# Conditioning vectors of a two-block transformer: from a TensorE product with a turn to a VectorE sum over weight blocks, closed by a product with ones

## The chip, the cores and the metric

One core of one Trainium2 chip runs the whole program. The metric is the device time of one launch in microseconds, the median of a few launches. The profile is of one more execution.

## The reference

The program runs a first block (four feed-forward layers around a pooling mixer and a differential attention) and then a second block (a Mamba mixer and an attention). The part that the change touches feeds the second block. Each of its two layers is modulated by vectors made from two conditioning vectors, one for the latent and one for the context rows:

```python
sc, scc = jax.nn.silu(c), jax.nn.silu(c_ctx)
for i in range(DEPTH):                                   # DEPTH = 2
    sh, scl, gt = jnp.split(sc @ mod_w[i] + mod_b[i], 3, axis=-1)
    shc, sclc, gtc = jnp.split(scc @ mod_w[i] + mod_b[i], 3, axis=-1)
    in_lat = rmsnorm_2(h_lat, norm_w[i]) * (1.0 + scl[:, None]) + sh[:, None]
    in_ctx = rmsnorm_2(h_ctx, norm_w[i]) * (1.0 + sclc) + shc
```

`c` and `c_ctx` have 1024 numbers, `mod_w[i]` is 1024 x 3072 in float32. So it is two rows times a matrix of 6144 columns in all: 25 MB of weights, each read once. Nothing before the Mamba mixer needs the result. The feed-forward layer that hides it is `h + 0.5 * (silu(n @ up_a) * (n @ up_b)) @ down`, with 512 rows and a hidden width of 2816.

## The kernel before

**Streams.** All large weights come through one stream of 438 units of 128 x 1024 float32 (512 KB, one block column of eight 128 x 128 blocks). SyncE loads a unit into one of two buffers `raw`; ScalarE copies it rounded into one of four buffers `wh` (`split`, line 1091); GpSimd computes the rest `wl = raw - wh` (line 392, one 128 x 1024 operation for each unit); TensorE then does three products for each block (high x high, high x low, low x high; `project`, line 469, 24 matmuls of 512 columns for a unit). Each engine runs its own instruction list in order. Semaphores connect them.

**The feed-forward loop.** The hidden width is done in parts of 8, 8 and 6 blocks. Over the blocks of a part runs a loop of w // 2 passes, with two pairs (`jj` = 0, 1) in each pass. A pair is two units: gate and value. So a pass with w = 8 has four units. The order on the engines in a pass is:

- TensorE: wait for `gated` (a PSUM bank is free), unit of the gate (unit 0 or 2 of the pass), unit of the value (unit 1 or 3);
- ScalarE: silu of the gate (line 1139), the splits of the units that take the places of the two just used, wait for `gated`, then the high half `fh` (line 1143);
- VectorE: wait for silu and for the value, product into `tmp` (line 1616, which signals `gated`), wait for `fh`, low half `fl` (line 1618).

Then the down projection of the part reads `fh` and `fl`, and line 1641 adds it to `x`.

**The modulation.** It rides in the loops of the first two parts of feed-forward layers 0, 1 and 2: 3 x 2 x 4 = 24 passes, each making 256 of the 6144 columns, for both rows. ScalarE issues two loads of 512 KB into `modw[:, 0]` and `modw[:, 1]` at the head of a pass (line 1137), after a wait that the buffers are free. In the second pair TensorE multiplies, between the two units, the eight 128-row chunks of the weights with the silu of the conditioning vectors (`csil`, padded to 32 columns), in four column groups of the array (line 516). VectorE copies the 128 x 256 result to `modst` (line 1603). Behind the last unit of the pass TensorE turns it into columns with two products against a selector `modsel` (line 525), which also adds the four groups. After the second part VectorE adds the bias to the 32 columns of the layer and stores them in `modv` (line 1627).

A float32 product counts as two TensorE instructions in the profile (line 516: 384 for 192 calls; line 525: 96 for 48), the rounded ones of `project` as one.

`link` is VectorE's own chain: `link.mark(ins)` lets an instruction count up a semaphore and `link.until(n)` waits for that count, so that an operation sees what an earlier one on the same engine wrote.

Of the kernel before, what the change touches and what calls it, by code (L numbers as in the profile page):

```python
# [27 lines left out]
P = 128  # L28
# [34 lines left out]
for _name, _n in STAGE_UNITS:  # L63
# [8 lines left out]
    ("m_d", 32), ("diff_lambda", 256), ("slopes", 8), ("pool_rcount", 64), ("modsel", 2),  # L72
]
COL = {}
NCOL = 0
# [34 lines left out]
def at(base, i=None, per=0):  # L110

    return base if i is None else i * per + base
# [7 lines left out]
def build(nc, A, ctx):  # L120
    def sb(name, shape, dt=FP32, scope=ctx):
        return scope.enter_context(nc.sbuf_tensor(name, shape, dt))

    def sem(name):
        return ctx.enter_context(nc.semaphore(name))
# [26 lines left out]
    with scope() as first:  # L152
        hh = sb("hh", [P, KD, T], F32R, first)
        hl = sb("hl", [P, KD, T], F32R, first)
        fh = sb("fh", [P, KD, T], F32R, first)
        fl = sb("fl", [P, KD, T], F32R, first)
        dist = sb("dist", [P, T], scope=first)
        csil = sb("csil", [P, KD, 32], scope=first)
        modw = sb("modw", [P, 2, UNIT], scope=first)
        mk = sb("mk", [P, 2 * X_HEADS, TC], scope=first)  # L160
        mv = sb("mv", [P, 2 * X_HEADS, 2, P], scope=first)
        with scope() as s:
            dq = sb("dq", [P, 2, T], scope=s)
            dk = sb("dk", [P, 2, T], scope=s)
            dv = sb("dv", [P, 2, T], scope=s)
            dvt = sb("dvt", [P, NB, P], scope=s)
            de = sb("de", [P, 2, 2, T], scope=s)
            dw = sb("dw", [P, T], scope=s)
            dT = sb("dT", [P, NB, T], scope=s)
            dnm = sb("dnm", [P, 2, 2], scope=s)  # L170
            drs = sb("drs", [P, 2, 2], scope=s)
            drr = sb("drr", [P, 2, 2], scope=s)
            drl = sb("drl", [P, 1], scope=s)
            lamt = sb("lamt", [P, 2, 64], scope=s)
            lams = sb("lams", [P, 2], scope=s)
            lame = sb("lame", [P, 2], scope=s)
            lam = sb("lam", [P, 1], scope=s)
            dgain = sb("dgain", [P, 1], scope=s)
        xoh = sb("xoh", [P, X_HEADS, T], F32R, first)
        xol = sb("xol", [P, X_HEADS, T], F32R, first)  # L180
        qx = sb("qx", [P, X_HEADS, T], scope=first)
        with scope() as s:
            ubuf = sb("ubuf", [P, 2, PAD + T], scope=s)
            sg = ubuf[:, :, 0:T]
            modst = sb("modst", [P, 2 * P], scope=s)
# [90 lines left out]
    s_init = sem("init")  # L276
    c_silu = sem("c_silu")
    mod_loaded = [sem(f"mod_loaded{s}") for s in range(2)]
    mod_acc, mod_staged = sem("mod_acc"), sem("mod_staged")
    mod_turned, mod_read, gmod_ready = sem("mod_turned"), sem("mod_read"), sem("gmod_ready")  # L280
# [52 lines left out]
    X0 = 2  # L333
# [123 lines left out]
    def _(pe):  # L457
# [48 lines left out]
                last = nc.tensor.matmul(B[6][:, chunk(c)], rstd[:, c:c + 1].to_broadcast([P, P]), ident, start=True, stop=True)  # L506
            last.then_inc(rb_ready, 1)

        def modulation(n, i):

            for s in range(2):
                pe.wait_ge(mod_loaded[s], at(16 * (n + 1), i, 16))
            for kk in range(2):
                for j in range(4):
                    k = 2 * j + kk
                    last = nc.tensor.matmul(B[6][32 * j:32 * j + 32, 2 * P:4 * P], csil[:, k, :],
                                            modw[:, k // 4, (k % 4) * 2 * P:(k % 4 + 1) * 2 * P],
                                            start=(kk == 0), stop=(kk == 1))
            last.then_inc(mod_acc, 1)

        def modulation_turn(n, i):

            pe.wait_ge(mod_staged, at(n + 1, i, 1))
            for h in range(2):
                last = nc.tensor.matmul(B[6][:, bass.ds(i * 4 + (4 * n + 2 * h) % 32 + 32 * (n // 8), 2)], modst[:, chunk(h)],
                                        col("modsel", 0, 2), start=True, stop=True)
            last.then_inc(mod_turned, 1)

        def ffn(f, name, norm, following):
            n = NORM[norm]  # L530
# [3 lines left out]
            for p, w in enumerate(FF_PARTS):  # L534
                def arrive(k):
                    pe.wait_ge(h_ready, 8 * n + k + 1)
                with pe.Fori(0, w // 2) as i:
                    for jj in range(2):

                        pe.wait_ge(gated, at(pairs + jj + 1, i, 2))  # L540
                        g = u + 2 * jj
                        project(g, hh, hl, [(B[2 * jj][:], 0, T)], i, 4, arrive=arrive if p == 0 and jj == 0 else None)
                        if w == KD and f < 3 and jj == 1:
                            modulation(8 * f + 4 * p, i)
                        project(g + 1, hh, hl, [(B[2 * jj + 1][:], 0, T)], i, 4)
                        if w == KD and f < 3 and jj == 1:
                            modulation_turn(8 * f + 4 * p, i)
                u += 2 * w
                done = xr(f, MIXERS_BEFORE[name]) + 8 * p
                hidden = pairs + w  # L550
# [532 lines left out]
    def _(act):  # L1083
# [41 lines left out]
        def ffn(f, name, norm_name, following, ready):  # L1125
# [3 lines left out]
            for p, w in enumerate(FF_PARTS):  # L1129
                with act.Fori(0, w // 2) as i:  # L1130
                    for jj in range(2):
                        g = u + 2 * jj
                        if w == KD and f < 3 and jj == 0:
                            n = 8 * f + 4 * p
# [303 lines left out]
        nc.scalar.activation(csil[:, :, 0:2], col("c", 0, 16).rearrange("p (k c) -> p k c", c=2), ACT.Silu).then_inc(c_silu, 1)  # L1438
# [122 lines left out]
    def _(dve):  # L1561
# [35 lines left out]
                    rest(k - 1)  # L1597
            rest(KD - 1)

        def modulation(n, i):  # L1600

            dve.wait_ge(mod_acc, at(n + 2, i, 1))
            nc.vector.tensor_copy(modst[:], B[6][:, 2 * P:4 * P]).then_inc(mod_staged, 1)

        def ffn(f, name, norm_name, gain):
            norm(norm_name, x, T, gain)
# [1 line left out]
            pairs = f * sum(FF_PARTS)  # L1608
            for p, w in enumerate(FF_PARTS):
                with dve.Fori(0, w // 2) as i:  # L1610
                    for jj in range(2):
                        if w == KD and f < 3 and jj == 1:
                            modulation(8 * f + 4 * p, i)
                        dve.wait_ge(silu_ready, at(pairs + jj + 1, i, 2))
                        dve.wait_ge(unit_done, at(u + 2 * jj + 2, i, 4))
                        nc.vector.tensor_tensor(tmp[:, jj, :], sg[:, jj, :], B[2 * jj + 1][:], ALU.mult).then_inc(gated, 1)  # L1616
# [2 lines left out]
                                                fh[:, bass.ds(i * 2 + jj, 1), :].bitcast(FP32), ALU.subtract)\  # L1619
                          .then_inc(hid_lo, 1)  # L1620
                        dve.wait_ge(hid_lo, at(pairs + jj + 1, i, 2))
                u += 2 * w

                if p == 1 and f < 3:

                    dve.wait_ge(mod_turned, 8 * (f + 1))
# [372 lines left out]


        nc.vector.memset(eps6[:], 1e-6)
        nc.vector.memset(csil[:], 0.0)
        nc.vector.memset(eps5[:], 1e-5).then_inc(s_init, 1)
        free = 0
        for signal, banks in ((gated, 2), (x_ready, X0), (kv_ready, 2), (kv_copied, 4), (mod_acc, 1)):
# [261 lines left out]
    return blocks  # L2267


def modulation_units(w):  # L2270

    w = w.reshape(2, 2, 4, P, 12, 2 * P).transpose(0, 4, 1, 3, 2, 5)
    return np.ascontiguousarray(w.reshape(48, P, UNIT))


# [44 lines left out]
```

## Time and profile before

| | us |
|---|---|
| median of 3 runs | 3976.95 (3973.89 to 3977.0) |
| profiled execution, its own time | 3973.89 |
| its span, first to last instruction | 3972.1 |

| engine | busy us | share |
|---|---|---|
| TensorE, matmul | 3600.4 | 91% |
| TensorE, weight load | 2925.1 | 74% |
| VectorE | 1547.8 | 39% |
| ScalarE | 1351.7 | 34% |
| GpSimd | 1245.0 | 31% |

The mean granted clock of TensorE is 0.938 of full speed. A row of the timeline gives the start of an instruction (or of a run of the same ones, with their count) and its duration; matmuls overlap, so the distance from start to start is the time that one costs. "Idle before" is how long the engine had stood still, and the name behind it who released it.

### The profile page before, as it was taken

To read this page: it belongs to the slowest core of one execution; us is meant where nothing else is said; L and a number is where in the kernel's file an instruction comes from. 1 tells how busy PE (TensorE), PEld (TensorE's weight loads), DVE (VectorE), ACT (ScalarE), POOL (GpSimd) and SP (SyncE) were. 2 spreads that over 40 slices of the span, in tenths; PEclk is the share of its full clock that TensorE was granted. 3 is DMA by queue.
4 is the path that set the end of the run, shared out by engine and by line. 5 is a ranking of instruction groups with operands and counts; after the bars stand their busy time and mean duration, and the time that the engine had idled before them with its cause. 6 is when DMAs were issued, how large, how long until landed. Compare 5 with 4: busy or idle time off the path is not lost.

```text
span 3972.1 us, 50085 instructions
## 1 busy us (share of the span) xinstructions
PE 3600.4 (91%) x17896; PEld 2925.1 (74%) x17896; DVE 1547.8 (39%) x2368; ACT 1351.7 (34%) x2246; POOL 1245.0 (31%) x683
## 2 busy tenths in 40 slices
PE   6999998999999998887999977899889897779998
PEld 6788876788878886565788866888878886646667
DVE  1322263322232224564322233665566665444442
ACT  3322233322232224444322233334333333324443
POOL 4244432344434442221244413333333423100001
PEclk9899999999999999998999979999999998779999
DMA  4333221233233321111122210100110101100001
GB/s 157 120 111 111 95 75 53 105 126 112 91 107 126 111 95 59 53 58 37 58 95 95 95 51 32 43 33 32 37 37 32 42 32 57 34 6 22 21 21 38
DMA packets 72964, 269.76 MB, mean 68 GB/s; under 512 B 8096, under 2 KB 8096, under 8 KB 72096
## 3 DMA queue, kind: packets, MB, share of 16 engines
q1 hardware_dynamic: 64944, 236.14, 17.8%
q10 hardware_dynamic: 7920, 32.25, 2.2%
q8 instruction: 68, 1.11, 0.1%
q14 instruction: 32, 0.26, 0.0%
HBM read 264.16 MB, written 4.19 MB: 68 GB/s over the span
## 4 chain that ended last, share of the span: by engine, by line
issue 46%; PE 29%; POOL 17%; DVE 5%; ACT 2%; POOLq 1%; ACTq 0%; DVEq 0%
POOL wl L392 15%; PE ps L469 13%; PE ps L915 2%; PE ps L897 2%; PE ps L482 1%; PE ps L924 1%; PE ps L494 1%; PE ps L483 1%; PE ps L484 1%; PE ps L784 1%; PE ps L797 1%; PE ps L834 1%; POOL xs L417 1%; DVE rstd L1791 1%; PE ps L898 1%
## 5 line engine op out<-in xcount | busy, mean ns | idle before, releaser
L392 POOL TENSOR_TENSOR wl<-raw,wh 128x1024 fp32r<-128x1024 f32 x438 | 1055.8, 2411 | 2585.0 <-ACT wh L1091 2585.0
L1091 ACT ACTIVATE wh<-raw 128x1024 fp32r<-128x1024 f32 x438 | 463.0, 1057 | 1200.2 <-PE ps L469 537.6
L469 PE MATMUL ps<-hh,wh 128*128 128x512 f32 (+1 forms) x1856 | 740.7, 399 | 30.7 <-DVE hl L1586 30.0
L469 PE MATMUL ps<-hl,wh 128*128 128x512 f32 (+1 forms) x1856 | 722.0, 389 | 0.0
L469 PE MATMUL ps<-hh,wl 128*128 128x512 f32 (+1 forms) x1856 | 721.9, 389 | 0.0
L469 PEld LDWEIGHTS ps<-hh,wh 128*128 128x128 f32 x1856 | 356.1, 192 | 140.6 <-issue 49.8
L469 PEld LDWEIGHTS ps<-hh,wl 128*128 128x128 f32 x1856 | 356.2, 192 | 75.0
L469 PEld LDWEIGHTS ps<-hl,wh 128*128 128x128 f32 x1856 | 357.4, 193 | 68.4 <-issue 1.7
L482 PE MATMUL ps<-fh,wh 128*128 128x512 f32 x768 | 306.3, 399 | 3.1 <-DVE fl L1618 3.0
L484 PE MATMUL ps<-fh,wl 128*128 128x512 f32 x768 | 300.8, 392 | 0.0
L483 PE MATMUL ps<-fl,wh 128*128 128x512 f32 x768 | 300.0, 391 | 0.0
L1616 DVE TENSOR_TENSOR tmp<-ubuf,ps 128x512 f32<-128x512 f32 x88 | 60.6, 689 | 600.4 <-PE ps L469 600.4
L1618 DVE TENSOR_TENSOR fl<-tmp,fh 128x512 f32 x88 | 206.9, 2351 | 92.6 <-ACT fh L1143 92.6
L469 PE MATMUL ps<-mh,wh 128*128 128x512 f32 (+1 forms) x768 | 217.8, 365 | 7.2 <-ACT cvin L1264 4.0
L1641 DVE SCALAR_TENSOR_TENSOR x<-ps,x 128x512 f32 (+1 forms) x96 | 65.6, 691 | 404.5 <-PE ps L484 404.5
L469 PE MATMUL ps<-ml,wh 128*128 128x512 f32 (+1 forms) x768 | 201.6, 344 | 0.0
L469 PE MATMUL ps<-mh,wl 128*128 128x512 f32 (+1 forms) x768 | 200.5, 343 | 0.0
L482 PEld LDWEIGHTS ps<-fh,wh 128*128 128x128 f32 x768 | 144.9, 189 | 34.4 <-DVE fl L1618 4.7
L484 PEld LDWEIGHTS ps<-fh,wl 128*128 128x128 f32 x768 | 144.4, 188 | 33.0
L483 PEld LDWEIGHTS ps<-fl,wh 128*128 128x128 f32 x768 | 144.7, 188 | 30.4
L1139 ACT ACTIVATE ubuf<-ps 128x512 f32<-128x512 f32 x88 | 52.6, 597 | 320.2 <-PE ps L469 320.2
L494 PE MATMUL ps<-sq,sqr 128*128 128x1 f32 x736 | 120.2, 294 | 33.7 <-ACT sqr L1098 33.3
(313 smaller groups left out, 5515.7 us busy)
## 6 DMA issues: line engine op xcount, KB each, us to landing
raw<-stream_dram SPq DMA_DIRECT2D x438, 512.0 KB, 3.2
modw<-mod_dram ACTq DMA_DIRECT2D x48, 512.0 KB, 3.6
x<-xT_dram SPq DMA_DIRECT2D x1, 2048.0 KB, 8.4
side<-ctxT_dram ACTq DMA_DIRECT2D x2, 1024.0 KB, 7.4
park_dram<-x ACTq DMA_DIRECT2D x1, 2048.0 KB, 8.4
x<-park_dram ACTq DMA_DIRECT2D x1, 2048.0 KB, 7.7
out_dram<-x SPq DMA_DIRECT2D x8, 256.0 KB, 2.2
side<-memT_dram SPq DMA_DIRECT2D x1, 1024.0 KB, 4.8
```

The source lines that it names most:

```text
L392: nc.gpsimd.tensor_tensor(wl[:, u % RING, :], raw[:, u % RAW, :], wh[:, u % RING, :].bitcast(FP32), ALU.subtract).then_inc(s_lo, 1)
L469: last = nc.tensor.matmul(bank, a[:, s, w], b[:, k, c0:c1], start=(k == 0 and a is wh and b is hi), stop=(k == KD - 1 and a is wl))
L482: nc.tensor.matmul(bank, wh[:, s, w], hi, start=start, stop=False)
L483: nc.tensor.matmul(bank, wh[:, s, w], lo, start=False, stop=False)
L484: last = nc.tensor.matmul(bank, wl[:, s, w], hi, start=False, stop=stop)
L494: last = nc.tensor.matmul(B[7][:, KD * c + k:KD * c + k + 1], sqr[:, k % 2, chunk(c)], ones[:, 0:1], start=True, stop=True)
L897: nc.tensor.matmul(ps[:, o:o + T], queries, kcur[h, to, 0:T], start=True, stop=True)
L915: last = nc.tensor.matmul(B[1][64 * r:64 * r + 64, b * P:(b + 1) * P], vcur2[:, k, :], pT2[:, s % 2, k, :], start=(k == 0), stop=(k == NCH ...
L1091: nc.scalar.activation(wh[:, u % RING, :], raw[:, u % RAW, :], ACT.Copy).then_inc(s_hi, 1)
L1616: nc.vector.tensor_tensor(tmp[:, jj, :], sg[:, jj, :], B[2 * jj + 1][:], ALU.mult).then_inc(gated, 1)
L1618: nc.vector.tensor_tensor(fl[:, bass.ds(i * 2 + jj, 1), :], tmp[:, jj:jj + 1, :], fh[:, bass.ds(i * 2 + jj, 1), :].bitcast(FP32), ALU.subt ...
L1641: nc.vector.scalar_tensor_tensor(x[:, m, :], B[4 + slot][:].unsqueeze(1), 0.5, x[:, m, :], ALU.mult, ALU.add).then_inc(x_ready, 1)
```

## The change

The modulation moves from products on TensorE to VectorE, and its weights are laid out in other units. For each block of 128 columns (48 of them, two in a pass) VectorE multiplies the eight 128 x 128 weight blocks each with one number for each partition and adds them up, once for each of the two rows: 16 operations of 128 x 128 for a block of columns, of which the first two are multiplications and the other 14 multiply-adds onto `modp`. TensorE adds over the partitions with one product against a column of ones for each row. In the pass:

- TensorE's products between the two units of the second pair are gone. Behind the last unit it waits twice for `mod_part`, each time for one block of columns, and does two products behind each wait.
- VectorE's copy to `modst` is gone. The 32 operations of a pass stand behind line 1618 of the first pair and ahead of line 1616 of the second. An operation waits for the one before last.
- ScalarE's wait ahead of the two loads is for `mod_used`, TensorE's last product of the pass before.

The amount loaded is the same, two units of 512 KB in a pass. `csil` loses its padding, its memset and its 32 columns.

```diff
 # TensorE
-        def modulation(n, i):
-            for s in range(2):
-                pe.wait_ge(mod_loaded[s], at(16 * (n + 1), i, 16))
-            for kk in range(2):
-                for j in range(4):
-                    k = 2 * j + kk
-                    last = nc.tensor.matmul(B[6][32 * j:32 * j + 32, 2 * P:4 * P], csil[:, k, :],
-                                            modw[:, k // 4, (k % 4) * 2 * P:(k % 4 + 1) * 2 * P],
-                                            start=(kk == 0), stop=(kk == 1))
-            last.then_inc(mod_acc, 1)
-        def modulation_turn(n, i):
-            pe.wait_ge(mod_staged, at(n + 1, i, 1))
-            for h in range(2):
-                last = nc.tensor.matmul(B[6][:, ...], modst[:, chunk(h)],
-                                        col("modsel", 0, 2), start=True, stop=True)
-            last.then_inc(mod_turned, 1)
+        def modulation(v, i):
+            pe.wait_ge(mod_part, at(2 * v + 2, i, 4))
+            for r in range(2):
+                last = nc.tensor.matmul(B[6][:, bass.ds(i * 4 + (2 * v + r), 1)], modp[:, v % 2, r, :], ones[:, 0:1],
+                                        start=True, stop=True)
+            last.then_inc(mod_used, 1)
...
                         project(g, hh, hl, [(B[2 * jj][:], 0, T)], i, 4, arrive=...)
-                        if w == KD and f < 3 and jj == 1:
-                            modulation(8 * f + 4 * p, i)
                         project(g + 1, hh, hl, [(B[2 * jj + 1][:], 0, T)], i, 4)
                         if w == KD and f < 3 and jj == 1:
-                            modulation_turn(8 * f + 4 * p, i)
+                            modulation(16 * f + 8 * p, i)
+                            modulation(16 * f + 8 * p + 1, i)
     # ScalarE
-                            act.wait_ge(mod_acc, at(n + 1, i, 1))
+                            act.wait_ge(mod_used, at(v + 2, i, 2))
                             for r in range(2):
-                                act.dma_start(modw[:, r:r + 1, :], A["mod"][at(2 * n + r, i, 2)].unsqueeze(1)).then_inc(mod_loaded[r], 16)
+                                act.dma_start(modw[:, r:r + 1, :], A["mod"][at(v + r, i, 2)].unsqueeze(1)).then_inc(mod_loaded[r], 16)
     # VectorE
-        def modulation(n, i):
-            dve.wait_ge(mod_acc, at(n + 2, i, 1))
-            nc.vector.tensor_copy(modst[:], B[6][:, 2 * P:4 * P]).then_inc(mod_staged, 1)
+        def modulation(v, i):
+            dve.wait_ge(mod_loaded[v % 2], at(16 * (v // 2 + 1), i, 16))
+            dve.wait_ge(mod_used, at(v + 1, i, 2))
+            done = {}
+            for k in range(KD):
+                for r in range(2):
+                    to, block, c = modp[:, v % 2, r, :], modw[:, v % 2, chunk(k)], csil[:, k, r:r + 1]
+                    if k:
+                        link.until(done[r])
+                        ins = nc.vector.scalar_tensor_tensor(to, block, c, to, ALU.mult, ALU.add)
+                    else:
+                        ins = nc.vector.tensor_scalar(to, block, c, None, ALU.mult)
+                    if k < KD - 1:
+                        done[r] = link.mark(ins)
+                    else:
+                        ins.then_inc(mod_part, 1)
...
                     for jj in range(2):
-                        if w == KD and f < 3 and jj == 1:
-                            modulation(8 * f + 4 * p, i)
                         dve.wait_ge(silu_ready, ...)
                         dve.wait_ge(unit_done, ...)
                         nc.vector.tensor_tensor(tmp[:, jj, :], sg[:, jj, :], B[2 * jj + 1][:], ALU.mult).then_inc(gated, 1)
...
+                        if w == KD and f < 3 and jj == 0:
+                            modulation(16 * f + 8 * p, i)
+                            modulation(16 * f + 8 * p + 1, i)
     # weights
-        "mod": modulation_units(I["mod_w_2"]),
+        "mod": units(outputs_first(I["mod_w_2"][0], 0, 24) + outputs_first(I["mod_w_2"][1], 0, 24)),
```

## Rows read from the trace of the kernel before

**Rows 1.** The page's first part: busy us (share of the span) xinstructions of each engine.

```profile
PE 3600.4 (91%) x17896; PEld 2925.1 (74%) x17896; DVE 1547.8 (39%) x2368; ACT 1351.7 (34%) x2246; POOL 1245.0 (31%) x683
```

**Rows 2.** Waits: engine line <- releaser: us in total, times, longest us.

```profile
DVE tmp L1616 <- PE ps L469: 600.4, 88, 10.2
```

**Rows 3.** Timeline of TensorE, first modulation: start us, us, line, [idle before <-releaser].

```profile
137.36 1.07 PE L516 MATMUL ps<-modw,csil 128*32 128x256 f32 x16
138.36 0.50 PE L469 MATMUL ps<-hh,wh 128*128 128x512 f32 x1
...
143.97 0.50 PE L525 MATMUL ps<-cols,modst 128*128 128x2 f32 x4
144.33 0.48 PE L469 MATMUL ps<-hh,wh 128*128 128x512 f32 x1
```

**Rows 4.** Timeline of VectorE over one pass of the first feed-forward loop.

```profile
131.97 0.69 DVE L1616 TENSOR_TENSOR tmp<-ubuf,ps 128x512 f32<-128x512 f32 x1 [6.55 <-PE ps L469]
133.71 2.35 DVE L1618 TENSOR_TENSOR fl<-tmp,fh 128x512 f32 x1 [1.06 <-ACT fh L1143]
...
144.17 0.69 DVE L1616 TENSOR_TENSOR tmp<-ubuf,ps 128x512 f32<-128x512 f32 x1 [5.25 <-PE ps L469]
...
155.62 0.69 DVE L1616 TENSOR_TENSOR tmp<-ubuf,ps 128x512 f32<-128x512 f32 x1 [7.35 <-PE ps L469]
```

**Rows 5.** Timeline of GpSimd over the same pass.

```profile
133.11 2.40 POOL L392 TENSOR_TENSOR wl<-raw,wh 128x1024 fp32r<-128x1024 f32 x1 [2.45 <-ACT wh L1091]
139.09 2.41 POOL L392 TENSOR_TENSOR wl<-raw,wh 128x1024 fp32r<-128x1024 f32 x1 [3.58 <-ACT wh L1091]
145.31 2.41 POOL L392 TENSOR_TENSOR wl<-raw,wh 128x1024 fp32r<-128x1024 f32 x1 [3.81 <-ACT wh L1091]
```

**Rows 6.** Timeline of ScalarE, the split behind the pass's last unit.

```profile
144.17 1.06 ACT L1091 ACTIVATE wh<-raw 128x1024 fp32r<-128x1024 f32 x1 [5.16 <-PE ps L469]
```

**Rows 7.** Timeline of VectorE, a pass of the loop that carries no modulation.

```profile
1409.99 0.69 DVE L1616 TENSOR_TENSOR tmp<-ubuf,ps 128x512 f32<-128x512 f32 x1 [10.18 <-PE ps L469]
...
1431.97 0.69 DVE L1616 TENSOR_TENSOR tmp<-ubuf,ps 128x512 f32<-128x512 f32 x1 [6.89 <-PE ps L469]
```

**Rows 8.** Groups by shape, VectorE: xcount | busy us, mean ns | idle before.

```profile
L1732 DVE SCALAR_TENSOR_TENSOR dw<-de,drr 128x128 f32<-128x128 f32 x8 | 2.8, 351 | 0.6
L1729 DVE TENSOR_SCALAR de<-de,drl 128x128 f32<-128x128 f32 x8 | 2.3, 286 | 0.3
```

**Rows 9.** Timeline of VectorE, differential attention: unchained ops, then a chained pair.

```profile
1533.99 0.61 DVE L1714 SCALAR_TENSOR_TENSOR de<-dist,cols,ps 128x128 f32<-128x128 f32 x2 [12.85 <-PE ps L655]
...
1571.64 0.16 DVE L1728 TENSOR_TENSOR drl<-drr,lam 128x1 f32<-128x1 f32 x1
1571.83 0.28 DVE L1729 TENSOR_SCALAR de<-de,drl 128x128 f32<-128x128 f32 x1
```

**Rows 10.** Timeline of VectorE, the convolution taps, each waiting for the op before last.

```profile
2656.50 1.01 DVE L1915 SCALAR_TENSOR_TENSOR sqr<-cvin,cols,sqr 128x770 f32<-128x770 f32 x1
2657.43 3.15 DVE L1915 SCALAR_TENSOR_TENSOR tmp<-cvin,cols,tmp 128x770 f32<-128x770 f32 x1
```

**Rows 11.** Timeline of GpSimd at the same time.

```profile
2657.21 2.55 POOL L392 TENSOR_TENSOR wl<-raw,wh 128x1024 fp32r<-128x1024 f32 x1 [1.74 <-ACT wh L1091]
```

**Rows 12.** Timeline of TensorE, its matmul behind a wait.

```profile
2673.26 1.01 PE L834 MATMUL ps<-yh,wh 128*128 128x512 f32 x2 [4.72 <-DVE acc L1998]
```

**Rows 13.** Stretches: TensorE busy (xinstructions), granted clock (1.00 is full), DMA share, GB/s.

```profile
2673.20:2675.80 2.60, 2.54 (x8) 0.50 0.43 162
2675.80:2676.80 1.00, 1.00 (x6) 0.75 0.00 0
...
1651.00:1655.00 4.00, 4.00 (x11) 0.50 0.34 112
1655.00:1656.50 1.50, 1.50 (x6) 0.76 0.13 52
```

**Rows 14.** DMA issues: xcount, KB each, median us to landing.

```profile
modw<-mod_dram ACTq DMA_DIRECT2D x48, 512.0 KB, 3.6
```

More of the change, by code:

```diff
@@ L71 @@
     ("m_norm_w", 16), ("a_q_norm", 1), ("a_k_norm", 1), ("c", 16), ("dt_bias", 64), ("a_log", 64),
-    ("m_d", 32), ("diff_lambda", 256), ("slopes", 8), ("pool_rcount", 64), ("modsel", 2),
+    ("m_d", 32), ("diff_lambda", 256), ("slopes", 8), ("pool_rcount", 64),
 ]
@@ L157, in build @@
         dist = sb("dist", [P, T], scope=first)
-        csil = sb("csil", [P, KD, 32], scope=first)
+        csil = sb("csil", [P, KD, 2], scope=first)
         modw = sb("modw", [P, 2, UNIT], scope=first)
@@ L184, in build @@
             sg = ubuf[:, :, 0:T]
-            modst = sb("modst", [P, 2 * P], scope=s)
+            modp = sb("modp", [P, 2, 2, P], scope=s)
         vt = modw[:, :, 0:TC]
@@ L278, in build @@
     mod_loaded = [sem(f"mod_loaded{s}") for s in range(2)]
-    mod_acc, mod_staged = sem("mod_acc"), sem("mod_staged")
-    mod_turned, mod_read, gmod_ready = sem("mod_turned"), sem("mod_read"), sem("gmod_ready")
+    mod_part = sem("mod_part")
+    mod_used, mod_read, gmod_ready = sem("mod_used"), sem("mod_read"), sem("gmod_ready")
     sq_ready, sq_used, rt_ready = sem("sq_ready"), sem("sq_used"), sem("rt_ready")
@@ L507, in norm_spread @@
             last.then_inc(rb_ready, 1)
-        def modulation(n, i):
-            for s in range(2):
-                pe.wait_ge(mod_loaded[s], at(16 * (n + 1), i, 16))
-            for kk in range(2):
-                for j in range(4):
-                    k = 2 * j + kk
-                    last = nc.tensor.matmul(B[6][32 * j:32 * j + 32, 2 * P:4 * P], csil[:, k, :],
-                                            modw[:, k // 4, (k % 4) * 2 * P:(k % 4 + 1) * 2 * P],
-                                            start=(kk == 0), stop=(kk == 1))
-            last.then_inc(mod_acc, 1)
-        def modulation_turn(n, i):
-            pe.wait_ge(mod_staged, at(n + 1, i, 1))
-            for h in range(2):
-                last = nc.tensor.matmul(B[6][:, bass.ds(i * 4 + (4 * n + 2 * h) % 32 + 32 * (n // 8), 2)], modst[:, chunk(h)],
-                                        col("modsel", 0, 2), start=True, stop=True)
-            last.then_inc(mod_turned, 1)
+        def modulation(v, i):
[4 more added lines that the diff above has]
+            last.then_inc(mod_used, 1)
         def ffn(f, name, norm, following):
@@ L1133, in ffn @@
                         if w == KD and f < 3 and jj == 0:
-                            n = 8 * f + 4 * p
-                            act.wait_ge(mod_acc, at(n + 1, i, 1))
+                            v = 16 * f + 8 * p
+                            act.wait_ge(mod_used, at(v + 2, i, 2))
                             for r in range(2):
-                                act.dma_start(modw[:, r:r + 1, :], A["mod"][at(2 * n + r, i, 2)].unsqueeze(1)).then_inc(mod_loaded[r], 16)
+                                act.dma_start(modw[:, r:r + 1, :], A["mod"][at(v + r, i, 2)].unsqueeze(1)).then_inc(mod_loaded[r], 16)
                         act.wait_ge(unit_done, at(g + 1, i, 4))
@@ L1437, in _ @@
         act.wait_ge(consts_in, 32)
-        nc.scalar.activation(csil[:, :, 0:2], col("c", 0, 16).rearrange("p (k c) -> p k c", c=2), ACT.Silu).then_inc(c_silu, 1)
+        nc.scalar.activation(csil[:].rearrange("p k c -> p (k c)"), col("c", 0, 16), ACT.Silu).then_inc(c_silu, 1)
         norm("ffn0", x, T, lambda k: (x_in, 16))
@@ L1610, in ffn @@
                 with dve.Fori(0, w // 2) as i:
+                    link.enter(i, 2 * 2 * (KD - 1) if w == KD and f < 3 else 0)
                     for jj in range(2):
-                        if w == KD and f < 3 and jj == 1:
-                            modulation(8 * f + 4 * p, i)
                         dve.wait_ge(silu_ready, at(pairs + jj + 1, i, 2))
@@ L1621, in ffn @@
                         dve.wait_ge(hid_lo, at(pairs + jj + 1, i, 2))
+                        if w == KD and f < 3 and jj == 0:
+                            modulation(16 * f + 8 * p, i)
+                            modulation(16 * f + 8 * p + 1, i)
+                    link.leave(w // 2)
                 u += 2 * w
                 if p == 1 and f < 3:
-                    dve.wait_ge(mod_turned, 8 * (f + 1))
+                    dve.wait_ge(mod_used, 2 + 16 * (f + 1))
                     nc.vector.tensor_tensor(modv[:, 16 * f:16 * f + 16], B[6][:, 32 * f:32 * f + 32].rearrange("p (m c) -> p m c", c=2),
@@ L2001, in _ @@
         nc.vector.memset(eps6[:], 1e-6)
-        nc.vector.memset(csil[:], 0.0)
         nc.vector.memset(eps5[:], 1e-5).then_inc(s_init, 1)
         free = 0
-        for signal, banks in ((gated, 2), (x_ready, X0), (kv_ready, 2), (kv_copied, 4), (mod_acc, 1)):
+        for signal, banks in ((gated, 2), (x_ready, X0), (kv_ready, 2), (kv_copied, 4), (mod_used, 2)):
             for _ in range(banks):
@@ L2267, in weight_stream @@
     return blocks
-def modulation_units(w):
-    w = w.reshape(2, 2, 4, P, 12, 2 * P).transpose(0, 4, 1, 3, 2, 5)
-    return np.ascontiguousarray(w.reshape(48, P, UNIT))
 def kernel(**inputs):
@@ L2294 @@
         "slopes": np.tile(np.array([2.0 ** (-8.0 * (h + 1) / DIFF_HEADS) for h in range(DIFF_HEADS)], f32), (P, 1)),
-        "modsel": (np.arange(P)[:, None] % 32 == np.arange(2)[None, :]).astype(f32),
         "pool_rcount": np.tile(np.concatenate([1.0 / np.minimum(np.arange(1, 17), w) for w in POOL_WINDOWS])
```

## The prediction

> **What bounds the kernel now.** I read the engines' busy shares first: TensorE's matmuls fill 91% of the span, VectorE 39% [rows 1]. The waits say the same of the feed-forward loops: in each of its 88 pairs VectorE stands waiting for a product of TensorE, 600.4 us in all [rows 2]. So whatever TensorE is spared there is gained, and whatever it has to wait for is lost.
>
> Then the timeline of one pass with a modulation. It lasts from one first-pair product at 131.97 to the next at 155.62: 23.65 us [rows 4]. A pass of the loop that carries none takes 1431.97 - 1409.99 = 21.98 us, two pairs of 10.99 [rows 7]. The modulation thus costs TensorE 1.67 us in each of its 24 passes, 40 us in all. Of it 1.00 lies between the start of the 16 instructions at line 516 and the next matmul, and 0.36 is the same distance for the 4 instructions at line 525 [rows 3].
>
> The reader should next see what line 1618 does in that pass. It is a 128x512 subtraction with both inputs in SBUF and takes 2.35 us, ending at 136.06; line 1616, of the same size with one input in PSUM, takes 0.69 [rows 4]. GpSimd's line 392 runs from 133.11 to 135.51 [rows 5]: line 1618 starts inside it and ends 0.55 after it. A VectorE operation on two SBUF tensors stands still while GpSimd's runs. All 32 added operations have their tensors in SBUF.
>
> **Part 1, what TensorE is spared.** The 16 instructions at line 516 go (1.00 us and the 0.31 around them that is left of the 1.67). The 4 at line 525 (0.36) become 8, in two groups of 4 of the same weight shape: 0.72. If TensorE never waited, a pass would be 21.98 + 0.72 = 22.7 us, 0.95 less than now, 23 us in 24 passes. This is the most that the change can give.
>
> **Part 2, what VectorE has to do.** In a pass 4 multiplications and 28 multiply-adds of 128x128. The trace has both shapes, from SBUF with a number for each partition: 286 and 351 ns [rows 8]. What one costs in a row is less than its duration: two such multiply-adds, not chained, take 0.61 us together, so the second comes 0.61 - 0.34 = 0.27 after the first [rows 9]. That holds with a wait for the operation before last, the form used here: taps of 1.01 us start 2657.43 - 2656.50 = 0.93 apart [rows 10]. So 0.266 for a multiply-add and 0.20 for a multiplication: 28 x 0.266 + 4 x 0.20 = 8.25 us a pass. This is the lower bound; above it is the full chain, duration plus 0.03 (0.16 us become 0.19 from start to start [rows 9]): 28 x 0.385 + 4 x 0.32 = 12.1 us. I take 8.25, since the taps have just this pattern.
>
> The Trainium skill, "VectorE: DVE Perf Modes", section "The DRAIN you can't avoid", says that the next operation does not start until the pipeline is empty. By this rule the cost from start to start would be the whole duration; the rows at hand show less, and the page itself lets an operation that is not held start earlier. It is the third rival below, whose price is worked out there from rows.
>
> **Part 3, when VectorE can do it.** Take times of the pass shown. The block starts at 136.15, behind line 1618. GpSimd's next line 392 comes at 139.09, for a unit whose use TensorE ended before the removed products, so it stays there [rows 5]. Does it get in between VectorE's operations, which follow without a gap? The taps say yes: GpSimd asked at 2657.21, took 2.55 instead of 2.40 us [rows 11], and the tap behind took 3.15 us instead of 1.01 [rows 10]. So VectorE loses 2.4 us and some 0.15 for the handover. TensorE now ends the pass's last unit 1.1 us earlier (about 142.95 against 144.05). ScalarE's split of 1.06 us follows at once [rows 6] and GpSimd's operation behind it: 144.2 to 146.6. VectorE isn't done (136.15 + 8.25 + 2.55 = 146.95) and loses another 2.55. **End: 149.5.**
>
> The Trainium skill, "SBUF — State Buffer", section "Who interferes with whom", calls this an exclusive lock held for a whole instruction and speaks against the change. It does not say who gets the lock next in a row of short operations; if VectorE kept it, the first rival below would hold.
>
> **Part 4, what waits.** TensorE's first wait (16 operations, done about 142.9) is met. It does 4 instructions to 143.3 and then stands in its second wait until 149.5: 6.2 us. Everything behind it in its list waits too, above all the next pass's four units. Line 1616 of the second pair, ready at 143, also comes only at 149.5, and with it lines 1143 and 1618 of that pair (done about 151.7) and, behind line 1143 on ScalarE, the two loads of the next pass (about 151 to 152). None of these is late again: TensorE needs that bank a whole unit later, the down projection needs the last half only after 18 matmuls, and the loads land in 3.6 us [rows 14] for use at about 167.
>
> The clock falls as well. Behind a standstill of 4.72 us TensorE came back [rows 12] at 0.50 and ran so until about 2676.3, for 3.1 us [rows 13]; in another place it ran at 0.50 until some 0.7 us past 1655.0, over 4.7 us of full load [rows 13]. At the 1.2 GHz level such a stretch does half of its work, so a loss of 1.55 us here, up to 2.4 there (3.3 if the half-loaded microseconds ahead of it counted in full). I take 1.6, and 0.5 instead of 0.36 for the four instructions behind the wait.
>
> **Sum of a pass:** 149.55 (semaphore seen) + 0.50 + two units 10.74 from first to last matmul start (10.95 less a step) + 0.43 to its end as line 1616 sees it + 1.6 = 162.8; less 131.97 = 30.85 us. Against 23.65 this is 7.2 more, times 24 = 173 us. The smaller memsets and the narrower constants are lost in rounding (one memset of 0.3 us, ahead of all work that is waited for). 3973.9, the profiled execution's own time, + 173 = **4147 us**. This execution lies 3 us under the median of the runs shown, which I leave inside the range.
>
> The point from which the change pays: VectorE done by 144.05 in this pass, so that 144.05 + 0.05 + 0.36 + 10.74 + 0.43 is 155.6. It is done 5.5 us later.
>
> **Rivals.**
> 1. *VectorE keeps SBUF.* GpSimd finds no gap in a row of operations 0.27 us apart. Then the end is 136.15 + 8.25 = 144.4, the standstill 1 us, the clock stays. Pass: 144.45 + 0.36 + 10.74 + 0.43 - 131.97 = 24.0 us, + 9 us: 3983. For it: the operations are shorter than the taps and leave no idle time. Against: the taps overlapped in the same way and GpSimd came in at the first change of operation.
> 2. *It is faster.* One mechanism: VectorE's block is hidden, all 32 operations by 143.3. Without GpSimd in between that needs 7.15 / 32 = 0.223 us each, with its operation at 139.09 only 0.14. Then the 23 us of part 1 are gained: 3951. For it only that the operations are short; the rows with this very shape say 0.27 at the least.
> 3. *Full duration or full chain.* An operation costs 0.35 to 0.385 us from start to start, 2.7 to 3.9 us more in a pass, all on the path: + 65 to 93 us on the forecast, 4212 to 4240. For it: 32 waits whose counts are computed in a loop. Against: the taps and the attention's pairs.
> 4. *The clock stays.* The standstill is there, the 1.2 GHz stretch isn't: 1.75 x 24 = 42 us less, 4105. Against it: the rows of the clock, where a shorter standstill was enough.
>
> **How the numbers follow.** Forecast 0.72 (with its own range 4120 to 4200: 0.02 us more for each operation is 15 us, a slow stretch of 6 us instead of 3 another 36), rival 4 0.08, rival 3 0.08, rival 1 0.06, rival 2 0.03, something else 0.03. The range 4085 to 4225 takes in rival 4 and the nearer end of rival 3. Under 0.2% (8 us) no change could be told here. Faster 0.03; same 0.03 (half of rival 1); slower 0.94.
>
> **What would show it.** In the profile after: a wait of TensorE or its weight loads for `modp` of VectorE, 24 times, some 6 us each, 150 us in all; distances of 30 to 31 us between line 1616's first products in these loops, 21.98 elsewhere; the new operations in rows of 11, 10 and 11 with one of some 2.7 us between the rows where GpSimd works; VectorE busy some 320 to 380 us more, GpSimd's line 392 slightly longer there; a granted clock of 0.5 for 3 us behind each wait. The prediction is wrong if GpSimd's operations wait for the whole block, if the multiply-adds come apart by other than 0.27 us, or if TensorE's slow stretch is much longer than 3 us.

## Result, and the profile after

The changed kernel takes 4106.8 us (median of 4 runs, 4105.76 to 4114.51); the kernel before takes 3975.6 (3973.89 to 3977.0). The ratio is 1.0334, with a 95% interval of 1.0319 to 1.0349: 131 us slower. The forecast was 4147 in a range of 4085 to 4225. The direction and the wait that makes it came as forecast. Of the two visits of GpSimd that VectorE's block of 32 operations was to suffer in a pass, only one came, and the forecast was 40 us too high, out of the 173 us that it gave as the loss.

The page's first part after the change, and three of its groups of instructions (execution count | busy us, mean ns | idle before), against [rows 1]:

```profile
PE 3644.1 (89%) x17608; PEld 2970.5 (72%) x17608; DVE 1762.2 (43%) x3112; ACT 1355.1 (33%) x2246; POOL 1330.4 (32%) x683
...
L392 POOL TENSOR_TENSOR wl<-raw,wh 128x1024 fp32r<-128x1024 f32 x438 | 1140.4, 2604 | 2642.0 <-ACT wh L1078 2642.0
...
L1615 DVE TENSOR_TENSOR tmp<-ubuf,ps 128x512 f32<-128x512 f32 x88 | 60.3, 686 | 553.5 <-PE ps L469 553.5
...
L1617 DVE TENSOR_TENSOR fl<-tmp,fh 128x512 f32 x88 | 179.2, 2036 | 89.9 <-ACT fh L1130 89.9
```

TensorE has 288 matmuls fewer and is busy 44 us longer: instructions went, and the ones behind the waits run at a lower clock. VectorE has 214 us more. GpSimd has the same 683 instructions and 85 us more: something makes its line 392 longer.

Two rows of the waits (engine, line <- releaser: us in total, times, longest us):

```profile
PE ps L513 <- DVE modp L1597: 90.2, 24, 5.6
...
DVE tmp L1615 <- PE ps L469: 553.5, 64, 12.5
```

TensorE now waits for VectorE once a pass, 24 times. VectorE's wait for a product is found 64 times instead of the 88 of [rows 2]: in 24 pairs the product is there first.

In what follows the block is VectorE's 32 operations of a pass, and a row of operations is a run of the same kind, one behind the other. The timeline of VectorE over the same pass as [rows 4] (start us, us, operation, [idle before <- releaser]):

```profile
133.29 0.69 DVE L1615 TENSOR_TENSOR tmp<-ubuf,ps 128x512 f32<-128x512 f32 x1 [6.54 <-PE ps L469]
135.04 2.36 DVE L1617 TENSOR_TENSOR fl<-tmp,fh 128x512 f32 x1 [1.05 <-ACT fh L1130]
137.61 0.48 DVE L1599 TENSOR_SCALAR modp<-modw,csil 128x128 f32<-128x128 f32 x2 [0.22 <-DVE fl L1617]
138.01 3.77 DVE L1597 SCALAR_TENSOR_TENSOR modp<-modw,csil,modp 128x128 f32<-128x128 f32 x14
141.69 2.72 DVE L1599 TENSOR_SCALAR modp<-modw,csil 128x128 f32<-128x128 f32 x2
144.33 3.75 DVE L1597 SCALAR_TENSOR_TENSOR modp<-modw,csil,modp 128x128 f32<-128x128 f32 x14
148.00 0.68 DVE L1615 TENSOR_TENSOR tmp<-ubuf,ps 128x512 f32<-128x512 f32 x1
...
162.40 0.69 DVE L1615 TENSOR_TENSOR tmp<-ubuf,ps 128x512 f32<-128x512 f32 x1 [11.55 <-PE ps L469]
```

The timeline of GpSimd over it, against [rows 5]:

```profile
134.43 2.41 POOL L392 TENSOR_TENSOR wl<-raw,wh 128x1024 fp32r<-128x1024 f32 x1 [2.44 <-ACT wh L1078]
140.41 3.71 POOL L392 TENSOR_TENSOR wl<-raw,wh 128x1024 fp32r<-128x1024 f32 x1 [3.56 <-ACT wh L1078]
145.41 4.89 POOL L392 TENSOR_TENSOR wl<-raw,wh 128x1024 fp32r<-128x1024 f32 x1 [1.29 <-ACT wh L1078]
```

Read the two together. GpSimd asks at 140.41, in the middle of the first 14 multiply-adds. They take 3.77 us, an undisturbed time (0.263 us from start to start). Only the two multiplications at 141.69 are long, 2.72 us instead of 0.48, and GpSimd's operation ends at 144.12, with them. It had stood for 1.3 us of its 3.71. It asks again at 145.41, and again the 14 multiply-adds are undisturbed: it ends at 150.30, 2.2 us after VectorE's block (144.33 + 3.75 = 148.08). So GpSimd got in once within the block, not twice. This holds for 22 of the 24 passes; the other two stand with experiment 3.

The timeline of TensorE, against [rows 3], and stretches of it, against [rows 13] (busy us (instructions), granted clock, DMA share, GB/s):

```profile
144.08 0.50 PE L513 MATMUL ps<-sq,modp 128*128 128x1 f32 x4
148.22 1.01 PE L513 MATMUL ps<-sq,modp 128*128 128x1 f32 x4 [3.64 <-DVE modp L1597]
149.09 0.77 PE L469 MATMUL ps<-hh,wh 128*128 128x512 f32 x1
```

```profile
138.00:145.00 7.00, 6.58 (x32) 1.00 0.21 73
145.00:146.60 1.60, 0.00 (x0) 0.90 0.82 238
146.60:148.20 1.60, 0.00 (x0) 0.50 0.22 90
148.20:153.00 4.80, 4.78 (x13) 0.50 0.53 198
153.00:162.00 9.00, 9.00 (x40) 0.99 0.21 71
```

TensorE stands for 3.64 us. The clock falls during this, and TensorE does the next 4.8 us at 0.50, the 1.2 GHz level. The next pass begins at 162.40: 29.11 us against 23.65 before. The other passes of these loops take 28.3 to 31.6.

### The profile page after: what moved, and what is told of

Its sections match the earlier page's. It is cut to its first block, busy times and chain, and to the rows that moved or that the text cites. A ratio compares the mean times of both kernels' runs of the same rounds, so it can differ in the third digit from the quotient of the medians.

```text
span 4107.7 us, 50989 instructions
## 1 busy us (share of the span) xinstructions
PE 3644.1 (89%) x17608; PEld 2970.5 (72%) x17608; DVE 1762.2 (43%) x3112; ACT 1355.1 (33%) x2246; POOL 1330.4 (32%) x683
## 4 chain that ended last, share of the span: by engine, by line
issue 47%; PE 28%; POOL 17%; DVE 5%; ACT 2%; POOLq 1%; ACTq 0%; DVEq 0%
POOL wl L392 15%; PE ps L469 12%; PE ps L902 2%; PE ps L884 2%; PE ps L482 1%; PE ps L911 1%; PE ps L494 1%; PE ps L483 1%; PE ps L484 1%; PE ps L771 1%; PE ps L784 1%; PE ps L821 1%; POOL xs L417 1%; DVE rstd L1794 1%; PE ps L885 1%
## 5 line engine op out<-in xcount | busy, mean ns | idle before, releaser
L392 POOL TENSOR_TENSOR wl<-raw,wh 128x1024 fp32r<-128x1024 f32 x438 | 1140.4, 2604 | 2642.0 <-ACT wh L1078 2642.0
L469 PE MATMUL ps<-hh,wh 128*128 128x512 f32 (+1 forms) x1856 | 754.4, 406 | 31.0 <-DVE hl L1573 29.6
L469 PE MATMUL ps<-hl,wh 128*128 128x512 f32 (+1 forms) x1856 | 739.9, 399 | 0.0
L469 PE MATMUL ps<-hh,wl 128*128 128x512 f32 (+1 forms) x1856 | 737.5, 397 | 0.0
L469 PEld LDWEIGHTS ps<-hh,wh 128*128 128x128 f32 x1856 | 367.0, 198 | 138.1 <-issue 40.5
L469 PEld LDWEIGHTS ps<-hh,wl 128*128 128x128 f32 x1856 | 365.7, 197 | 77.5
L469 PEld LDWEIGHTS ps<-hl,wh 128*128 128x128 f32 x1856 | 367.8, 198 | 73.5 <-issue 1.7
L1617 DVE TENSOR_TENSOR fl<-tmp,fh 128x512 f32 x88 | 179.2, 2036 | 89.9 <-ACT fh L1130 89.9
L1597 DVE SCALAR_TENSOR_TENSOR modp<-modw,csil,modp 128x128 f32<-128x128 f32 x672 | 184.5, 349 | 0.0
```

Of the source, the lines that this page charges most:

```text
L392: nc.gpsimd.tensor_tensor(wl[:, u % RING, :], raw[:, u % RAW, :], wh[:, u % RING, :].bitcast(FP32), ALU.subtract).then_inc(s_lo, 1)
L469: last = nc.tensor.matmul(bank, a[:, s, w], b[:, k, c0:c1], start=(k == 0 and a is wh and b is hi), stop=(k == KD - 1 and a is wl))
L1597: ins = nc.vector.scalar_tensor_tensor(to, block, c, to, ALU.mult, ALU.add)
L1617: nc.vector.tensor_tensor(fl[:, bass.ds(i * 2 + jj, 1), :], tmp[:, jj:jj + 1, :], fh[:, bass.ds(i * 2 + jj, 1), :].bitcast(FP32), ALU.subt ...
```

## The experiments

Each edit is shown against the changed kernel, with what is left out marked by three dots. Theory A1, formed on the rows above, says that VectorE's multiply-adds, each of which starts before the one ahead of it has ended, keep GpSimd out of SBUF, and that it gets in only where such a row is broken or over.

**1. The eight products one pass later.** TensorE multiplies in each pass what VectorE summed in the pass before.

```diff
     # TensorE, gate and up projections
-                        if w == KD and f < 3 and jj == 1:
+                        if w == KD and f < 3 and jj == 0:
...
     # and behind the second part's down projection
+                        modulation(16 * (f + 1), None)
+                        modulation(16 * (f + 1) + 1, None)
...
     # VectorE
-            dve.wait_ge(mod_used, at(v + 1, i, 2))
+            dve.wait_ge(mod_used, at(v - v % 2 + 2 + 2 * (v // 16), i, 2))
...
     # ScalarE, the loads
-                            act.wait_ge(mod_used, at(v + 2, i, 2))
+                            act.wait_ge(mod_part, at(2 * v + 4, i, 4))
```

The read of the sums moves behind the down projection's adds, its columns shift by one pass, and `modp` is cleared at the start of each layer.

> VectorE's 32 operations of a pass are unchanged and stand where the change put them. TensorE does its four products with ones one pass later, behind the second unit of the next pass's first pair (the last ones of a layer behind the second part's down projection), ScalarE's loads wait for VectorE's end instead of TensorE's. Theory A (all of the loss is TensorE standing in the wait for VectorE's block, and the clock behind it): the wait is gone, a pass is 21.98 + 0.72 = 22.7 us against 23.65 before the change, 23 us less in 24 passes: about 3952 us (3945 to 3968). Rival C (the loss is in what the block does to the others: GpSimd's delayed operations, the late first product of the second pair): the time stays over 4040. Between the two, 3975 to 4040, if the block hides but ScalarE's later silu takes its place.

Measured: 3965.1 us (9 runs), ratio to before 0.9978 (0.9967 to 0.9988). The timeline of VectorE:

```profile
132.46 0.69 DVE L1620 TENSOR_TENSOR tmp<-ubuf,ps 128x512 f32<-128x512 f32 x1 [6.55 <-PE ps L469]
...
155.34 0.69 DVE L1620 TENSOR_TENSOR tmp<-ubuf,ps 128x512 f32<-128x512 f32 x1 [5.28 <-PE ps L469]
```

No wait of TensorE for `modp` is left, and the clock stays at 1.00 there. VectorE's block is as long as in the change (10.4 us), now beside TensorE's work; a pass takes 22.88 us. So the whole loss hangs on the wait. It came out 13 us over the expectation. A pass is 0.18 us longer than 22.7, 4 us in all, and the waits show more:

```profile
PE ps L482 <- DVE fl L1622: 9.0, 10, 1.2
```

Before the change this wait is 3.0 us in 4 times. The 6 that are new, some 6.0 us, are one for each of the six parts: the second pair's `fl` of the last pass is late for the down projection, since the block, with GpSimd in it, ends late even here. With the shorter block of experiment 7 they are gone. Some 3 of the 13 us stay open.

**2. Half the operations, each 256 wide.** Both units of a pass are multiplied in one operation.

```diff
-                    to, block, c = modp[:, v % 2, r, :], modw[:, v % 2, chunk(k)], csil[:, k, r:r + 1]
+                    to, block, c = modp[:, :, r, :], modw[:, :, chunk(k)], csil[:, k, r:r + 1]
...
-                            modulation(16 * f + 8 * p + 1, i)
```

> The change with both column blocks in one operation: 16 operations of 128x256 a pass instead of 32 of 128x128, 2 multiplications and then 14 multiply-adds; TensorE waits once for all. By the rows of before one takes 483 ns, 0.40 from start to start, so the block is 14 x 0.40 + 2 x 0.27 = 6.1 us instead of the 8.3 of the change without GpSimd. Theory A1 (in a row of multiply-adds VectorE keeps SBUF and GpSimd's operation gets in only at the two multiplications or at the end): the block runs from 137.6 to 143.8 of the pass shown, TensorE hardly waits, no slow clock: a pass of 22.8 to 23.3, 3952 to 3968 us. Theory B (GpSimd gets in between any two, as I predicted): 2.5 us more, a wait of 2 to 2.5 us, 4010 to 4070 us according to the clock.

Measured: 3959.7 us (7 runs), ratio 0.9964 (0.9952 to 0.9975). The timelines of VectorE and of GpSimd:

```profile
135.80 0.62 DVE L1600 TENSOR_SCALAR modp<-modw,csil 128x256 f32<-128x256 f32 x2 [0.31 <-DVE fl L1618]
136.33 5.63 DVE L1598 SCALAR_TENSOR_TENSOR modp<-modw,csil,modp 128x256 f32<-128x256 f32 x14
142.39 0.69 DVE L1616 TENSOR_TENSOR tmp<-ubuf,ps 128x512 f32<-128x512 f32 x1 [0.43 <-PE ps L469]
```

```profile
138.52 8.57 POOL L392 TENSOR_TENSOR wl<-raw,wh 128x1024 fp32r<-128x1024 f32 x2 [3.57 <-ACT wh L1078]
```

There is one row of multiply-adds and no break in it. GpSimd asks at 138.52, 3.4 us before the row ends, and two of its operations, 4.8 us of work, take 8.57. VectorE is done 10.6 us after the pass's start, 0.2 us before TensorE is through the pass's last unit, and no wait of TensorE for `modp` is left. The work costs 0.40 us for 256 columns and 0.263 for 128.

**3. The four multiplications first, then 28 multiply-adds of 128x128.** The work is that of the change; the break in the row is gone.

```diff
...
+            steps = [(s, 0, r) for s in range(2) for r in range(2)]
+            steps += [(s, k, r) for s in range(2) for k in range(1, KD) for r in range(2)]
+            for s, k, r in steps:
...
```

> The change with one order altered: the four multiplications of a pass first, then the 28 multiply-adds. Same operations, same waits on TensorE. Theory A1 (GpSimd gets in only at a multiplication): it is kept out of the whole block, which ends at 137.6 + 8.3 = 145.9 instead of 148.0; TensorE waits 1.8 us instead of 3.9. Without a slow clock a pass is 24.2 us, 3990 us; with the slow stretch of the change (2.4 us a pass) 4045. Theory B (it gets in wherever it asks): 4100 to 4150 us, as the change or above.

Measured: 4036.0 us (4 runs), ratio 1.0154 (1.0137 to 1.0171). VectorE, GpSimd, TensorE in the same pass:

```profile
137.24 7.44 DVE L1599 SCALAR_TENSOR_TENSOR modp<-modw,csil,modp 128x128 f32<-128x128 f32 x28
144.60 0.67 DVE L1617 TENSOR_TENSOR tmp<-ubuf,ps 128x512 f32<-128x512 f32 x1
```

```profile
139.17 10.51 POOL L392 TENSOR_TENSOR wl<-raw,wh 128x1024 fp32r<-128x1024 f32 x2 [3.58 <-ACT wh L1078]
```

```profile
144.82 0.84 PE L513 MATMUL ps<-sq,modp 128*128 128x1 f32 x4 [1.48 <-DVE modp L1599]
```

GpSimd is kept out for the whole row, 5.4 us, and the block lasts 8.15 us, the 8.25 of the prediction's part 2. Moving two multiplications thus took 71 us off the change. TensorE still stands for 1.48 us, and the clock still falls in a part of the passes. In the pass shown:

```profile
144.60:148.00 3.40, 3.18 (x10) 0.56 0.34 107
148.00:154.00 6.00, 6.00 (x20) 0.68 0.82 289
```

The timeline gives the length of 15 passes in which GpSimd stays out, this one included: 7 take 24.8 to 25.1 us and 8 take 26.4 to 27.9; the clock stays at 1.00 behind the wait in a short one (172.6 to 182) and falls in the next, a long one (0.80 from 197.6 to 201).

The rule has exceptions. In 3 of the 24 passes GpSimd got in twice within such a row, and the 28 took 11.66 us:

```profile
285.44 11.66 DVE L1599 SCALAR_TENSOR_TENSOR modp<-modw,csil,modp 128x128 f32<-128x128 f32 x28
...
287.37 3.56 POOL L392 TENSOR_TENSOR wl<-raw,wh 128x1024 fp32r<-128x1024 f32 x1 [3.58 <-ACT wh L1078]
292.37 2.48 POOL L392 TENSOR_TENSOR wl<-raw,wh 128x1024 fp32r<-128x1024 f32 x1 [1.45 <-ACT wh L1078]
```

These are the first passes of three of the six loops: of the second part in layers 0 and 1, and of the first part in layer 2. In the change GpSimd got in a second time within the second row of 14 in two passes, the first of the second part in layer 0 and of the first part in layer 2, 31.56 and 31.35 us long. What is different there stays open.

**4. The wait filled.** TensorE does 16 matmuls of 128x512 that nothing needs, into a bank that is free, between its two groups of products.

```diff
                             modulation(16 * f + 8 * p, i)
+                            for k in range(16):
+                                nc.tensor.matmul(B[4][:], hh[:, k % KD, 0:P], hh[:, k % KD, :], start=True, stop=True)
                             modulation(16 * f + 8 * p + 1, i)
```

> The change with 16 idle matmuls of 128x512 (3.65 us, written to an unused bank, results dropped) on TensorE between the products of the pass's first and second column block, that is in the stretch in which it stands waiting (3.64 us). The wait as such stays. Theory A: the granted clock stays at 1.00, the 2.4 us that the slow stretch costs a pass and 0.15 of the slow products go: 24 x 2.5 = 60 us less than the change, 4047 us (4035 to 4060). If the clock costs nothing, the time stays at 4107.

Measured: 4059.9 us (4 runs), ratio 1.0214 (1.0196 to 1.0231). TensorE's timeline and its stretches (columns as before):

```profile
143.11 3.93 PE L535 MATMUL ps<-hh 128*128 128x512 f32 x16
146.88 0.58 PE L513 MATMUL ps<-sq,modp 128*128 128x1 f32 x4
```

```profile
142.50:147.00 4.50, 4.50 (x24) 1.00 0.32 117
147.00:152.00 5.00, 4.77 (x24) 1.00 0.58 205
152.00:158.00 6.00, 6.00 (x28) 1.00 0.25 91
```

VectorE's first product of the next pass:

```profile
158.98 0.69 DVE L1617 TENSOR_TENSOR tmp<-ubuf,ps 128x512 f32<-128x512 f32 x1 [9.47 <-PE ps L469]
```

VectorE's block is unchanged to 0.02 us, TensorE gets on no earlier in the pass (14.92 us after its start, in the change 14.93), and a pass is 27.02 instead of 29.11. More work made the kernel 47 us faster. The slow clock is therefore 47 of the change's 131 us. The other 84 are the wait itself, less what TensorE is spared: counted from experiment 1, where nothing waits for `modp`, the change loses 142 us, 47 by the clock and 95 by the wait.

**5. Each operation waits for the one before.** The same operations in the same order, without overlap.

```diff
+                    if done:
+                        link.until(max(done.values()))
                     if k:
-                        link.until(done[r])
```

> The change with one alteration: each of the 16 operations of a column block waits for the one directly before it instead of the one before last, so that none overlaps its neighbour. One then costs its duration plus 0.03 us: 28 x 0.38 + 4 x 0.31 = 11.9 us a pass without GpSimd. Theory D (GpSimd gets in where VectorE's operations don't overlap, which is why it was kept out of the rows of multiply-adds): both of its operations of the pass get in where they ask, each takes about 2.5 us, VectorE's block ends at 137.6 + 11.9 + 5.0 = 154.5, a pass is 35.3 us, about 4254 us. Theory A1 (only at a multiplication): one gets in, the other waits to the end, 32.8 us a pass, about 4195 us.

Measured: 4227.4 us (2 runs), ratio 1.0641 (1.0621 to 1.0660). The timelines of VectorE and of GpSimd:

```profile
137.89 7.30 DVE L1598 SCALAR_TENSOR_TENSOR modp<-modw,csil,modp 128x128 f32<-128x128 f32 x14
145.11 2.69 DVE L1600 TENSOR_SCALAR modp<-modw,csil 128x128 f32<-128x128 f32 x2
147.83 5.26 DVE L1598 SCALAR_TENSOR_TENSOR modp<-modw,csil,modp 128x128 f32<-128x128 f32 x14
```

```profile
140.05 2.41 POOL L392 TENSOR_TENSOR wl<-raw,wh 128x1024 fp32r<-128x1024 f32 x1 [3.57 <-ACT wh L1078]
145.05 2.34 POOL L392 TENSOR_TENSOR wl<-raw,wh 128x1024 fp32r<-128x1024 f32 x1 [2.60 <-ACT wh L1078]
```

GpSimd gets in as soon as it asks, both times at its full speed. The second visit falls on the break between the rows; the first lies within a row, as it does in all 24 passes. So it is the overlap that keeps it out, not that VectorE was there first. The time is 27 us under the 4254 that was expected for this case: a visit costs VectorE some 2.0 us (7.30 - 5.26) instead of 2.5.

**6. The row of experiment 2 at 512 columns.** The operations work on twice the columns, half of them of other blocks; the sums are not those of the reference, and `modp` is 512 columns wide. There is one run, so no interval.

```diff
-                    to, block, c = modp[:, v % 2, r, :], modw[:, v % 2, chunk(k)], csil[:, k, r:r + 1]
+                    to, block, c = modp[:, r, :], modw[:, k // 2 % 2, k % 2 * T:(k % 2 + 1) * T], csil[:, k, r:r + 1]
```

> The modulation's sums are computed on wrong shapes here (the result is not the reference's): VectorE's block is 2 multiplications and 14 multiply-adds of 128x512 in the order and with the overlaps of the 256-wide experiment, 14 x 0.665 + 2 x 0.41 = 10.1 us a pass. The question is only whether GpSimd gets in. Theory W (it gets in between wide operations, as at the convolution taps of 770 columns, and not between narrow ones): it gets in at the first change of operation after it asks, twice a pass, its operations take 2.4 to 3 us, the block 15 us, the time is about 4215 us. Theory A1/D (overlapping operations keep it out at any width): its operations take up to 8 us, the block stays at 10.1 us, about 4100 us.

Measured: 4227.2 us. The timelines of VectorE and of GpSimd:

```profile
137.30 13.60 DVE L1598 SCALAR_TENSOR_TENSOR modp<-modw,csil,modp 128x512 f32<-128x512 f32 x14
```

```profile
139.22 2.41 POOL L392 TENSOR_TENSOR wl<-raw,wh 128x1024 fp32r<-128x1024 f32 x1 [3.58 <-ACT wh L1078]
144.23 2.81 POOL L392 TENSOR_TENSOR wl<-raw,wh 128x1024 fp32r<-128x1024 f32 x1 [2.59 <-ACT wh L1078]
```

The operations overlap here too (they come 13.60 / 14 = 0.97 us apart and last 1.04 in the mean), and GpSimd gets in at once. Overlap alone doesn't do it: the operations must be narrow, or short, as well; the two are not told apart. That fits the taps of 770 columns [rows 10, 11], from which the prediction read its rule and which had let it in.

**7. Experiments 1 and 2 together.** The edits are those above.

> Both repairs together: 16 operations of 128x256 on VectorE and TensorE's products one pass later. Theory A: nothing waits for VectorE in the loop, and since its block of 6.1 us ends before the second pair's product is due, the low half of the last block isn't late for the down projection either, as it was with the products later alone (10 waits of 9.0 us). A pass of 22.75 us, 0.9 less than before the change and 0.3 less than with 256-wide operations alone: 3950 to 3956 us, 5 to 10 us under the 256-wide one. Rival: what is left there is TensorE's own work, both are equal within 3 us, about 3959.

Measured: 3955.7 us (5 runs), ratio 0.9960 (0.9946 to 0.9973), passes of 22.88 us, no wait of TensorE for `modp`, and for `fl` only the 3.0 us that it had before the change. The intervals of this one and of experiment 2 overlap, so it isn't shown that the later hand-over still adds something. Both beat the two kernels: 0.4% under before, 3.6 to 3.7% under the change.

## Why the prediction was right, and where its size came from

The change is slower because TensorE stands behind `modp`, as predicted: without that wait the same operations give 0.9978 (experiment 1). By the steps:

- **Part 1, what TensorE is spared.** The most was put at 0.95 us a pass, 23 us. With nothing to wait for, a pass is 22.88 (experiments 1 and 7), 0.77 less than before, 18 us; experiment 7 gave back 16 (11 to 21). The eight products cost 0.8 to 0.9 us where 0.72 was taken: in experiment 1 TensorE's next unit comes 0.81 behind them.
- **Part 2, VectorE's work.** 8.25 us was right: 28 x 0.263 and twice 0.40 make 8.16. One of its two sources was misread: line 1714's pair [rows 9] has an input in PSUM and is not "such" a multiply-add; the cost came out the same. The third rival (the whole duration for each operation) is refuted in this order of waits: 14 operations whose mean is 349 ns take 3.77 us. Where each waits for the last, its 0.385 holds at once (experiment 5: 5.26 / 14 = 0.376, and the last of the 14 waits only for the one before last).
- **Part 3, when VectorE can do it: the term that was mis-sized.** "Does it get in between VectorE's operations, which follow without a gap? The taps say yes". It gets in at the change from one row to the next, and, in 22 of the 24 passes, not within a row of 128x128. The block was put at 8.25 + 2 x 2.55 and lasts 10.39 = 8.16 + 2.2. VectorE is done 14.71 us into the pass instead of 17.53.
- **The first rival** (GpSimd finds no gap) had the right rule for most passes and the wrong place for it, because the change has two rows with a break between them. Experiment 3 takes the break away. Its 3983 still came out as 4036: the standstill is 1.48 us instead of 1 and is enough to bring the clock down in a part of the passes, and in three passes GpSimd got in twice all the same.
- **Part 4, what waits.** The standstill is 3.64 us instead of 6.2. What follows was put too low. From TensorE's next unit to the next pass it is 162.40 - 149.09 = 13.31 us; before, and in experiment 4 at full clock (158.98 - 147.69), it is 11.29. So the slow stretch costs 2.0 us instead of 1.6: it lasts 4.8 us behind the wait, not 3.1. The four products behind it, with their way to the next unit, take 0.87 us (149.09 - 148.22) instead of 0.50, and in experiment 4, at full clock, still 0.81: they cost more in that place than the 0.36 of the four of [rows 3], and the clock is not why. "None of these is late again" held in the change; in experiment 1, where nothing else covered it, the second pair's `fl` was, by some 6 us more than before the change.
- **The sum.** VectorE done at 14.71, 0.22 until TensorE goes on, 0.87 and 13.31 make 29.11. The forecast has 17.53, 0.05, 0.50 and 12.77 in their place, 30.85. GpSimd's second visit was 2.8 us too much, the terms behind the wait 1.1 too little: 1.7 x 24 = 42 us, near the 40 from 4147 to 4106.8. Two terms erred in opposite ways, so by luck the total came out nearer than its largest term.
- **The fourth rival** put the slow clock at 42 us; experiment 4 shows 47 (2.0 x 24 = 48 from the pass).
- **The signs to look for.** 24 waits came, of 3.8 us in the mean where 6 was expected; the clock of 0.50 came and lasted longer. Rows of 11, 10 and 11 did not: the rows are of 14 and 14. VectorE's +214 us is under the 320 to 380, since each second visit of GpSimd lies outside the block; there it makes the `fl` at line 1617 shorter too, 2.04 us in the mean. Of the three things that would prove the prediction wrong, two came in part: GpSimd's second operation of a pass waits for the end of the block, and the slow stretch is 4.8 us instead of 3. The multiply-adds are 0.263 us apart, as forecast.

What is left open: by what rule the chip orders VectorE and GpSimd (the runs show at which widths and waits, at four points); what in the break lets GpSimd in, the change of operation or that the multiplications wait for nothing; and why GpSimd got in within a narrow row in a few passes, each the first of its loop.

## What to carry to other kernels

A step moved to an idle engine is free only if its result is ready when the bounding engine asks; compare the end of the block with the point of use, and if it is late, hand over one pass later, or do the step in fewer and wider operations, before giving the move up. Count in the block what the other engine on the same memory adds, and look for it at the breaks in a row of operations. A short standstill of TensorE costs more than itself: here 3.64 us of it cost 2.0 us more in the slow work behind.

## What was not expected of the hardware

- A row of overlapping float32 multiply-adds from SBUF of 128 or 256 columns on VectorE kept GpSimd's SBUF operation out until the row ended: 2.41 us of work took 4.89, two of them 10.51. At 128 columns a few passes were exceptions (2 of 24 in the change, 3 of 24 in experiment 3). At 512 columns the same operation took 2.41 and 2.81 us, and with each operation of 128 columns waiting for the last 2.41 and 2.34.
- 16 idle matmuls (3.93 us) in TensorE's wait made the kernel 47 us faster, for the clock stayed at 1.00.
- The clock fell behind a standstill of 1.48 us too, in a part of the passes (0.56 and 0.68 in the stretches behind it in the first), much shorter than the 4.72 of [rows 12].
